# Two transformer blocks on one Trainium2 core: loads of weights, modulation and a transform matrix in another order around the merge and down stages

## What is computed

```python
mod = silu_c @ w_mod[layer] + b_mod[layer]
sh1, sc1, g1, sh2, sc2, g2 = [m[:, None, :] for m in jnp.split(mod, N_MOD, axis=-1)]
h = modulate(rms_norm(x, norm1_w[layer]), sh1, sc1)
q, k, v, g, f = split_proj(h @ wi)
o, _, _ = bidir_retention(q, k, v, a_f, a_b, s_f, s_b)
# fourier_mix: z = fft2(f as (l, 4, 128), axes=(1, 3), norm='ortho').real, then z @ w_four_out
y = merge_branches(h, ret_readout(o, g, w_ret_out[layer]),
                   fourier_mix(f, w_four_out[layer]),
                   w_branch_gate[layer], b_branch_gate[layer], w_out[layer])
# merge_branches: gates = sigmoid(h @ w_bg + b_bg); (g_r * ret_d + g_f * four_d) @ w_out
x = x + g1 * y
h2 = modulate(rms_norm(x, norm2_w[layer]), sh2, sc2)
x = x + g2 * conv_ffn(h2, w_up[layer], conv_w[layer], conv_b[layer], w_down[layer])
# conv_ffn: u = depthwise_conv3(h @ w_up); a, val = split(u); (gelu(a) * val) @ w_down
```

## Time and profile before

| | |
|---|---|
| median of 3 runs | 2527.25 us (2525.51 to 2527.36) |
| profiled execution | 2529.91 us, span 2528.1 us |
| mean granted TensorE clock | 0.965 of full |
| PE busy | 2333.3 us, 92% |
| DVE, ACT, POOL busy | 896.2 us (35%), 618.4 us (24%), 133.9 us (5%) |
| chain that ended last | PE 72%, DMA 20%, DVE 4%, ACT 2% |
| data moved | 570.11 MB, mean 226 GB/s |

### The profile page before, as it was taken

The page is one execution under the profiler, slowest core; times in us unless marked ns, Lnnn a source line. Parts: engine busy times, 40 slices in busy tenths (PEclk is TensorE's granted clock), DMA queues, the critical chain, the costliest instruction groups (busy, mean ns, idle before and its releaser), DMA issues.

```text
span 2528.1 us, 25780 instructions
## 1 busy us (share of the span) xinstructions
PE 2333.3 (92%) x11168; PEld 1525.9 (60%) x11168; DVE 896.2 (35%) x1177; ACT 618.4 (24%) x873; POOL 133.9 (5%) x128
## 2 busy tenths in 40 slices
PE   6999999999998999998999997998988989898988
PEld 5874878777886787876668786433343434343434
DVE  4837445535677424544642433010100000010102
ACT  5215133233333225414542321000000000000001
POOL 0221000110000002120000020000000000000000
PEclk8999999999999999999999997999999999999998
DMA  7220445325455222220002234999999999999993
GB/s 266 100 78 1 148 142 184 108 100 175 158 200 200 101 100 102 99 75 34 1 1 100 100 133 170 415 428 428 427 428 428 428 428 427 428 428 428 428 428 167
DMA packets 116823, 570.11 MB, mean 226 GB/s; under 512 B 5390, under 2 KB 28215, under 8 KB 92135
## 3 DMA queue, kind: packets, MB, share of 16 engines
q1 hardware_dynamic: 115104, 564.21, 55.7%
q0 software_dynamic: 1200, 4.13, 0.5%
q10 hardware_dynamic: 407, 0.13, 0.0%
HBM read 566.35 MB, written 2.10 MB: 225 GB/s over the span
## 4 chain that ended last, share of the span: by engine, by line
PE 72%; DMA 20%; DVE 4%; ACT 2%; issue 1%; POOL 1%; ACTq 0%; SPq 0%; DVEq 0%; POOLq 0%
PE ps L755 42%; DMA arena<-in_w_exp_up 9%; PE ps L1285 8%; PE ps L1348 6%; DMA arena<-in_w_exp_gate 6%; PE ps L1268 3%; DMA weights<-in_w_exp_gate 2%; PE ps L1171 1%; PE ps L1189 1%; DMA arena<-in_w_exp_down 1%; PE ps L1129 1%; PE ps L992 1%; PE ps L1300 1%; PE ps L1148 1%; DMA weights<-in_w_mod 1%
## 5 line engine op out<-in xcount | busy, mean ns | idle before, releaser
L755 PE MATMUL ps<-weights_r 128*128 128x512 f32 (+1 forms) x2784 | 861.9, 389 | 14.8 <-DVE weights_r L1874 5.0
L755 PEld LDWEIGHTS ps<-weights_r 128*128 128x128 f32 x2784 | 522.3, 189 | 128.6 <-issue 16.9
L755 PE MATMUL ps<-hT_r,weights_r 128*128 128x512 f32 x1264 | 463.0, 391 | 0.5 <-DVE weights_r L1874 0.5
L1285 PE MATMUL ps<-weights,arena 128*64 128x512 f32 x768 | 353.5, 617 | 60.1 <-DMA weights<-in_w_exp_up 46.3
L1287 PE MATMUL ps<-weights,arena 128*64 128x512 f32 x768 | 354.3, 618 | 0.0
L1874 DVE TENSOR_TENSOR weights_r<-weights,weights_r 128x4096 fp32r<-128x4096 f32 (+1 forms) x47 | 201.5, 4288 | 284.2 <-ACT weights_r L1433 282.4
L1285 PEld LDWEIGHTS ps<-weights,arena 128*64 128x64 f32 x768 | 105.9, 142 | 288.4 <-issue 286.5
L755 PEld LDWEIGHTS ps<-hT_r,weights_r 128*128 128x128 f32 x1264 | 238.6, 189 | 51.9 <-issue 2.2
L1433 ACT ACTIVATE weights_r<-weights 128x4096 fp32r<-128x4096 f32 (+1 forms) x47 | 165.3, 3518 | 339.5 <-PE ps L755 144.2
L755 PE MATMUL ps<-arena_r,weights_r 128*128 128x512 f32 (+1 forms) x640 | 228.6, 394 | 15.0 <-DVE weights_r L1874 15.0
L2473 DVE TENSOR_TENSOR hT<-hT,ps 128x512 f32<-128x512 f32 x32 | 22.0, 688 | 464.0 <-PE ps L1287 464.0
(11 more groups left out here) (290 smaller groups left out, 2511.5 us busy)
## 6 DMA issues: line engine op xcount, KB each, us to landing
weights<-in_w_exp_gate SPq DMA_DIRECT2D x48, 2048.0 KB, 23.1
weights<-in_w_exp_up SPq DMA_DIRECT2D x48, 2048.0 KB, 27.1
weights<-in_w_exp_down SPq DMA_DIRECT2D x48, 2048.0 KB, 27.0
weights<-in_w_in SPq DMA_DIRECT2D x18, 2048.0 KB, 7.9
arena<-in_w_exp_gate SPq DMA_DIRECT2D x16, 2048.0 KB, 27.6
arena<-in_w_exp_up SPq DMA_DIRECT2D x16, 2048.0 KB, 28.5
arena<-in_w_exp_down SPq DMA_DIRECT2D x16, 2048.0 KB, 28.4
weights<-in_w_mod SPq DMA_DIRECT2D x12, 2048.0 KB, 8.1
```

The lines of the kernel that those rows point to most:

```text
L755: last = pe.matmul(t, a if w_first else b, b if w_first else a, start=(k == 0 and n == 0), stop=(k == kt - 1 and n == len(pairs) - 1))
L1285: la = pe.matmul(bank(b0 + n)[0:64, :], xe[:, 2 * j + r, 0:64], wa[:, r, n * 512:(n + 1) * 512], start=start, stop=stop)
```

## The change

1. *DFT matrix.* It is no chunk any more. POOL loads it to a place of its own in the arena (`dft_cols`), ahead of the small matrix; PE waits for both before `fa` instead of for the small one before `z`. `prepare("dft")` goes on ACT and DVE.
2. *Modulation chunks of the merge.* Chunk 6 + i stands behind gate chunk i (before: 6 ahead of the first, then 7 + i), 10 behind out1's first chunk, 11 behind its second. DVE sums chunk 6 + i in the step in which PE turns it; PE turns 10 after tile 3 of out1 and 11 after tile 6.
3. *out1 and second norm.* ACT rounds up chunk 0 after the square of tile 4, and does the SiLU of the second block's modulation after that of tile 6. DVE's residual tiles, sums, columns and `prepare` are ordered anew. Up chunk 1 is rounded and subtracted in two halves right after the norm's scale (`half_high`, `half_low`, which now serve in2's chunk 1 too).
4. *Down.* Modulation chunk 11 of the second block stands behind down chunk 0, so down 0 stands directly behind modulation 10 and is split with the last up chunk. The first `act_rest` is done within the last up step.
5. The experts' first loads take the slots in the order in which the last chunks are spent.

```diff
@@ -158,7 +158,7 @@
                 b.add((tag, kind, part, nq, n), "A" if kind == "gate" else "D")
-            if tag == "m1" and i < 5:
+            if tag == "m1" and i < 4:
                 b.add(("mod1", "T", 6 + i), "D")
...
@@ -213,8 +213,8 @@
         b.add(("out1", n), "D")
-        if n == 3:
-            b.add(("mod1", "T", 11), "D")
+        if n in (3, 6):
+            b.add(("mod1", "T", 10 + (n == 6)), "D")
     norm("n2")
...
@@ -413,30 +413,28 @@
         mod1(5)
-        chunk("dft", dft_len)
-        mod1(6)
         for i, (kind, part, nq) in enumerate(MERGE):
...
             if kind == "gate":
-                mod1(7 + i)
+                mod1(6 + i)
         def mod2(i):
...
             chunk(("out1", nq), kmaj(w_out[0], 512 * nq, 512 * nq + 512))
-            if nq == 0:
-                mod1(11)
+            mod1(10 + nq)
         for j in range(UPN):
...
             mod2(j)
-        mod2(11)
         for j in range(6):
...
                 chunk(("down", j), part)
+                if j == 0:
+                    mod2(11)
             else:
...
@@ -486,7 +483,7 @@
 
-        last_tile = {"dft": ("fa", 3, 1), ("down", 5): ("cT2", 3),
+        last_tile = {("down", 5): ("cT2", 3),
                      ("in1", 0): ("qk1", 3), ("in1", 1): ("qk1", 7), ("in1", 2): ("v", 0, 3),
...
@@ -589,6 +587,7 @@
         dftd = at(13312, 2, P)
+        dft_cols = at(14336, 2, 768)
 
...
@@ -715,9 +714,9 @@
             load(0, SLOTS)
-            for m in range(RAW):
-                wait_spent(sp, NCH - RAW + m)
-                load(0, m)
+            for n in range(NCH - RAW, NCH):
+                wait_spent(sp, n)
+                load(0, n % RAW)
             for i in sorted(range(len(split) - 2, len(split)), key=high_slot):
...
@@ -923,11 +922,13 @@
                 if tag == "out1":
-                    mod_turn("mod1", 11)
+                    mod_turn("mod1", 10)
                 else:
...
                     feature_tiles((tag, 1), [(tag, n)], x, c0=n % 4 * P)
+                    if tag == "out1" and n == 6:
+                        mod_turn("mod1", 11)
                     for k in {4: (0, 1, 2), 5: (3,), 6: (4,), 7: (5,)}[n]:
...
@@ -1032,18 +1033,17 @@
             mod_turn("mod1", 4)
-            wl = slots[landed(pe, "dft")][:, 0:1536].rearrange("p (m n) -> p m n", m=2)
+            pe.wait_ge(S["dist_in"], 64)
             for g in range(FG):
...
                         o = c0 if k < 2 else 256
-                        last = pe.matmul(t[:, o:o + n], f_tok[:, k, g * P:(g + 1) * P], wl[:, m, c0:c0 + n],
+                        last = pe.matmul(t[:, o:o + n], f_tok[:, k, g * P:(g + 1) * P], dft_cols[:, m, c0:c0 + n],
                                          start=(k != 3), stop=(k != 2))
...
             mod_turn("mod1", 5)
-            pe.wait_ge(S["dist_in"], 48)
             for g in range(FG):
...
@@ -1431,6 +1429,19 @@
                     A(slots_r[high_slot(i)][:, 0:n], slots[sl][:, 0:n], ACT.Copy).then_inc(S["high_ready"], 1)
+
+            def half_high(kind, i, q):
+
+                at_split = split.index(chunk_at[kind, i])
+                if q == 0:
+                    landed(act_e, (kind, i))
+                    wait_spent(act_e, split[at_split - 2])
+                c = slice(q * SLOT // 2, (q + 1) * SLOT // 2)
+                A(slots_r[high_slot(at_split)][:, c], slots[split[at_split] % RAW][:, c], ACT.Copy).then_inc(
+                    S["quarter_high"], 1)
+                if q == 1:
+                    act_e.wait_ge(S["quarter_high"], QUARTERS[kind, i] + 2)
+                    act_e.sem_inc(S["high_ready"], 1)
 
...
@@ -1625,13 +1635,22 @@
             prepare(("out1", 0))
-            act_e.wait_ge(S["mod_summed"], summed_mods("mod1", 11))
-            mod_silu(3)
-            prepare(("out1", 1))
-            norm_squares(2, "n2", xT, L, lambda k: wait_freed(act_e, ("out1", k)))
+            def between_out1(k):
+
+                if k == 4:
+                    prepare(("out1", 1))
+                if k == 6:
+                    act_e.wait_ge(S["mod_summed"], summed_mods("mod1", 11))
+                    mod_silu(3)
+                    A(small[:, 1:2], eps_col, ACT.Sqrt)
+
+            norm_squares(2, "n2", xT, L, lambda k: wait_freed(act_e, ("out1", k)), after=between_out1)
             act_e.wait_ge(S["mods_ready"], 2)
...
                         h_parts[0], 2)
+            half_high("up", 1, 0)
+            half_high("up", 1, 1)
+            issued[0] += 1
             mod_rows("mod2", 0)
...
@@ -1673,19 +1692,7 @@
                 if q == 3:
-                    act_e.wait_ge(S["quarter_high"], 4)
-                    act_e.sem_inc(S["high_ready"], 1)
-
-            def second_high(q):
-
-                if q == 0:
-                    landed(act_e, ("in2", 1))
-                    wait_spent(act_e, split[first_in2 - 1])
-                c = slice(q * SLOT // 2, (q + 1) * SLOT // 2)
-                A(slots_r[high_slot(first_in2 + 1)][:, c], slots[split[first_in2 + 1] % RAW][:, c], ACT.Copy).then_inc(
-                    S["quarter_high"], 1)
-                if q == 1:
-                    act_e.wait_ge(S["quarter_high"], 6)
+                    act_e.wait_ge(S["quarter_high"], QUARTERS["in2", 0] + 4)
                     act_e.sem_inc(S["high_ready"], 1)
...
@@ -1875,6 +1882,18 @@
 
+            def half_low(kind, i, q):
+
+                at_split = split.index(chunk_at[kind, i])
+                ve.wait_ge(S["quarter_high"], QUARTERS[kind, i] + q + 1)
+                c = slice(q * SLOT // 2, (q + 1) * SLOT // 2)
+                sl = split[at_split] % RAW
+                last = ve.tensor_tensor(slots_r[sl][:, c], slots[sl][:, c],
+                                        slots_r[high_slot(at_split)][:, c].bitcast(F32), ALU.subtract)
+                if q == 1:
+                    ve.wait_ge(S["high_ready"], at_split + 1)
+                    last.then_inc(S["low_ready"], 1)
+
             def low_h(nth, k, high, low, src):
...
@@ -2019,13 +2038,12 @@
                         if i < 4:
-                            mod_sum("mod1", 7 + i)
-                        if i < 5:
+                            mod_sum("mod1", 6 + i)
                             mod_columns("mod1", 6 + i)
...
                 if tag == "m1":
-                    mod_sum("mod1", 11)
+                    mod_sum("mod1", 10)
 
...
@@ -2044,9 +2062,15 @@
                 if tag == "out1":
+                    mod_columns("mod1", 10)
+                    residual([(tag, 4)], 16, cc, 4)
+                    mod_sum("mod1", 11)
+                    residual([(tag, n) for n in (5, 6)], 16, cc, 5)
+                    prepare((tag, 1))
                     mod_columns("mod1", 11)
-                else:
-                    free("rbias", "D", ve.tensor_copy(route_bias, wait_full(ve, "rbias")[:, 0:NE]))
+                    residual([(tag, 7)], 16, cc, 7)
+                    return
+                free("rbias", "D", ve.tensor_copy(route_bias, wait_full(ve, "rbias")[:, 0:NE]))
                 residual([(tag, 4)], 16, cc, 4)
...
@@ -2168,8 +2192,6 @@
             mod_columns("mod1", 4)
-            prepare("dft")
-            mod_sum("mod1", 6)
             mod_columns("mod1", 5)
...
@@ -2180,6 +2202,9 @@
             norm_scale(2, "n2", xT, hT, L, split_h=(2, *h_parts))
+            half_low("up", 1, 0)
+            half_low("up", 1, 1)
+            issued[0] += 1
             def act_rest(k0):
...
@@ -2201,6 +2226,8 @@
                         prepare(("up", j))
+                    if (j, n) == (UPN - 1, 1):
+                        act_rest(0)
                 wait_freed(ve, ("up", j, 3))
...
@@ -2208,7 +2235,6 @@
                     mod_columns("mod2", j - 1)
-            act_rest(0)
             mod_columns("mod2", 10)
...
@@ -2555,6 +2570,7 @@
             po.wait_ge(S["g_ready"], KT)
+            po.dma_start(dft_cols[:, :, :], dft_len).then_inc(S["dist_in"], 16)
             po.dma_start(dftd[:, :, :], dft_dim).then_inc(S["dist_in"], 16)
...
             def sum_squares(m):

```

More of the change, by code:

```diff
@@ L451, in build_two_blocks @@
         order = {n: name for name, n in chunk_at.items()}
-        assert NCH % RAW == 0
         split = [n for n, name in enumerate(chunk_at)
@@ L546, in build_two_blocks @@
         first_in2 = split.index(chunk_at["in2", 0])
+        QUARTERS = {("up", 1): 0, ("in2", 0): 2, ("in2", 1): 6}
         root, recip = small[:, 40:44], small[:, 44:48]
@@ L1398, in norm_root, with norm_squares @@
                 copy_out(tag, root[:, 0:width // P], ACT.Sqrt, width=width // P, bias=bias)
-            def norm_squares(m, tag, src, width, written=None, between=None):
+            def norm_squares(m, tag, src, width, written=None, after=None):
                 A(small[:, 4:5], eps_col, ACT.Sqrt)
-                square_tiles(m, src, width, written)
-                if between:
-                    between()
+                square_tiles(m, src, width, written, after=after)
```

(19 more changed lines are left out.)

## The result

Over 20 runs each, the changed kernel takes 2530.57 us (2527.38 to 2534.33), the kernel before 2526.98 us (2522.68 to 2530.65): ratio 1.0017, 95% interval 1.001 to 1.0024, that is +4.3 us (+2.5 to +6.1; the two medians as they stand differ by 3.6). The direction is the one forecast and the measured time lies in the range; but the size, forecast as +8.0, is about half, and at 0.17% it is a difference that the forecast's own bound of 0.2% calls none.

A forecast was written before the change was run, and what follows sets the result against it. PE bounds the kernel, busy for most of the span and waiting for weights at full DMA rate in the second block's experts. Terms 3.4 + 8.0 + 9.4 − 3.7 − 9.1 = +8.0 give 2535.3 us, range 2526.5 to 2542.5.

The forecast's parts named there:

- A: First block's DFT: wait before turn 5 goes, a wait before the DFT comes; +3.4 us, bounds +1.5 and +7.
- B: Merge, turn 7: PE waits 5.5 us for its sum, plus 2.5 for the clock; +8.0 us, bounds +5 and +8.5.
- C: Merge, turn 9: PE waits for its sum, projection b0 starts later; +9.4 us, bounds +8 and +10.5.
- D: Second norm and up: modulation chunk 0 lands late, up chunk 1's wait goes; −3.7 us, bounds −5 and −0.5.
- E: Down stage: down chunk 0 loaded earlier, PE's wait before it shrinks; −9.1 us, bounds −8 and −10.
- rival 2: No change: gate b0 3 us sooner, clock not falling for so short a wait; total +0.8 us, 2528.0; chance 0.15.
- The rule on issuing engines: DMA transfers begun by different engines share the same 16 engines; the matrix load by POOL adds 1.8 us to gate a0.
- The forecast's case: Whole kernel slower by +4.5 to +12 us, around the term sum of +8.0; chance 0.64.
- The rival of quick pairs: Faster: the second load of each pair lands within some 9 us; sum −8.5 us, median 2518.7; chance 0.10.
- Rival 3: Slower still: slow stretches last through z, halves of up 1 wait for a load; +14.8 us, 2542; chance 0.09.
- rival 4: DFT matrix, asked for late by POOL, lands after 315 and fa waits for it; another +5 us; chance 0.02.

The follow-up runs named there:

- turns one step later: Changed kernel with turns and columns of modulation 6 to 9 one merge step later; ratio 0.9953 to the kernel before, −16.2 us against the changed kernel.
- filling the waits: Changed kernel with added matmuls keeping PE at work before turns 7 and 9; ratio 0.9994 to the kernel before, −5.8 us against the changed kernel.
- the last kernel of the experiments: Kernel before with down 0 early, up 1 in halves, DFT matrix loaded by POOL, modulation 6 ahead of gate a0; 2504.76 us, ratio 0.9908.
- the kernel with both repairs: Changed kernel with turns of modulation 6 to 9 one merge step later and gate a0 split behind the f tiles; ratio 0.9913 to the kernel before.
- Down alone: Kernel before with only the down part: modulation 11 behind down chunk 0, first lows of act within the last up step; ratio 0.9961, −9.9 us.

## Why the prediction was right in direction and too large

**The places** were all right: a wait before the DFT, before turn 7 and before turn 9, none before turn 5 and up chunk 1, a shorter one before down 0. No other wait of PE in these parts changed by more than about 1.4 us.

**A** is the term that was mis-sized most: +1.4, not +3.4. Gate a0 was ready 0.6 us sooner than worked out (issued 278.45, landed 293.81, 15.4 us; I had 14.2 + 1.8 = 16.0), and DVE's pieces behind it took 0.2 us less. The 14.2 was counted from the issue of the pair's first load (353.60); gate b0 itself was issued at 354.55 and landed after 13.25 us. The larger part is the step "It starts it behind a long wait: +2.5". The chain of the changed kernel:

```profile
278.45 15.34 DMA weights<-in_w_branch_gate
293.81 3.64 ACT weights_r L1431
...
309.75 12.99 PE ps L1043 x64
322.74 0.79 PE ps L835 x8
```

The granted clock was at 0.50 well before the wait ended (0.50 over 304.00 to 309.70) and back at full by about 314 (0.94 over 314 to 316). Under it, PE first ran the four matmuls of the DFT's first piece, which take tokens that are ready sooner, while DVE did the last sums of f (to 311.52). A slow clock there costs nothing. The main piece began at 311.58 and ended with the DFT at 322.74: 11.2 us, where it took 9.88 in the kernel before. That is 1.3 us, not 2.5. The wait was counted up to the main piece and the clock's loss whole behind it: the same microseconds twice.

**B and C** were right within 0.4 us (+8.4 and +9.3), in the mechanism too: the turns one step later bring back 16.2 us, filling the waits brings 2.4 and 2.5. That sum 8 would be ready in time is right as well.

**D** came out at −4.9, not −3.7. The up chunks took 43.98 us together against the 44.8 worked out, since the slow stretch was over with the wait and the step for modulation 0 (clock 0.51 over 559.90 to 566.30, 0.99 over the two chunks). And that step began 8.0 us after out1's end (554.77 to 562.73), where 8.4 were assumed for the load alone. PE waited 1.43 us for POOL's squares instead of 2.08, but that gained nothing, since the load ended last. That the new order of squares costs nothing is right.

**E** was −8.4, not −9.1: DVE's last pieces behind up chunk 10 ended at 828.6 and PE began at 828.9, where the same sum, shifted by 11.5 us with the rest, gives 828.1. The wait of 7.5 us in the prediction doesn't follow from its own sum (14.98 − 9.1 = 5.9); 6.64 was measured. The down stage itself was 0.8 us shorter, which the sentence "so the slow stretch behind it stays and is no gain" had at 0: in the 8 us from the start of the down stage the clock was 0.74, against 0.64 before, since less of the slow stretch was left when the wait ended.

Two slips don't change the forecast: A's lower bound is +1.6, and rival 2 adds up to +0.6, not +0.8.

So the term sum was +8.0 and the traces show +5.9, with errors of −2.0 (A), +0.4, −0.1, −1.2 (D) and +0.7 (E), which partly cancel (rounded); the down stage brings it to +5.1, and the runs say +4.3 with a width of 1.8 us on each side. What lies between the last two isn't resolved.

**The rule on issuing engines** (the Trainium skill, "DMA: Bandwidth & Descriptors", section "Issuing engines are not separate DMA queues"): POOL issued the matrix at 280.26, 1.8 us behind gate a0, and gate a0 took 15.36 us from issue to landing against 14.00 for b0, which had only one load beside it. In the six profiled executions that have both pairs, gate a0 took 15.1 to 15.4 us and b0 14.0 to 14.4: the trace agrees with the rule, and the matrix (with the small one behind it) cost gate a0 about 1.1 us, not 1.8. No run has gate a0 in this place without the matrix, so this is a comparison of two pairs. By it, on a path of its own the matrix would have left the wait about 1 us shorter.

**The chances.** The forecast's case began at +4.5, the measured difference is +4.3 with +6.1 as upper end; 0.18 for "no difference" was too little for a sum of five terms of both signs, each with an error of one or two microseconds, whose result stood only 3 us above the bound. That the difference came out so small is not rival 2's doing: the waits before turns 7 and 9 were met in full and paid for. The rival of quick pairs is out: from its own issue, gate b0 as second of a pair took 13.2 to 14.4 us in the nine executions that have that pair, and down chunk 0 13.9. Rival 3 is out (clock 1.00 over z, up chunk 1 split in time), and so is rival 4: the matrix landed 7.6 us after POOL issued it at 280.26, long before the DFT.

## What to carry to other kernels

An engine's instruction that waits for another's sum should be placed where that sum is done by the latest load ahead of it, not where its number fits: shifting turns by one step was worth 16 us, the order of the merge's loads nothing (at the down stage, where PE waited for the load itself, moving it forward was worth most of 10 us). A wait costs its own length and the slow clock behind it, but only as far as the slow work is on the path: the clock falls within a long wait, and what of the slow stretch passes before PE's next needed work is free. Where it overlaps another wait it must not be counted again. Before moving a chunk forward in a list, look at what the splitting helper pulls ahead of whom.

## What the runs showed that was not expected

Two waits of nearly the same length, at the same instruction (the sequence behind the fifth in-projection), left different clocks. The kernel before, timeline of PE and window:

```profile
175.36 1.26 PE L984 MATMUL ps<-arena 64*128 64x512 f32 x4 [2.04 <-issue]
```

```profile
175.20:186.20 11.00, 10.84 (x34) 4.84 (x36) 6.31 (x11) 4.38 (x10) 7.96 (x15) 0.84 0.48 181
```

The changed kernel, whose program is the same there:

```profile
174.30 1.13 PE L985 MATMUL ps<-arena 64*128 64x512 f32 x4 [1.88 <-issue]
```

```profile
174.20:185.20 11.00, 10.90 (x42) 4.92 (x44) 7.36 (x12) 4.38 (x10) 8.40 (x15) 1.00 0.50 187
```

A wait of 2.04 us was followed by a slow stretch, one of 1.88 us by none, which moved all that follows by 1.7 us between two executions. It isn't the length that decides. At the same place, waits in the last kernel of the experiments and in "Turns one step later", each with its window:

```profile
175.32 2.50 PE L985 MATMUL ps<-arena 64*128 64x512 f32 x8 [1.93 <-issue]
...
175.20:186.20 11.00, 10.88 (x34) 4.86 (x36) 6.31 (x11) 4.38 (x10) 8.29 (x15) 0.84 0.49 185
```

```profile
176.05 1.99 PE L985 MATMUL ps<-arena 64*128 64x512 f32 x8 [2.42 <-issue]
...
175.90:186.90 11.00, 10.85 (x42) 4.87 (x44) 7.41 (x13) 4.38 (x10) 8.48 (x15) 1.00 0.46 177
```

The shorter of these was followed by a slow stretch, the longer by none. Over the ten profiled executions this place had a slow stretch in three (waits of 1.93, 2.04 and 2.39 us) and none in seven (1.79 to 2.42 us). The wait of 1.33 us for the lows of the branch was followed by a mean clock of 0.72 over 6 us in "Turns one step later" and in the kernel with both repairs, and by 1.00 in the kernel before, in "Down alone" and in the last kernel. What decides in these cases is open; no experiment was made on it.

From the f tiles to the down stage every wait of 4.7 us and more was followed by a slow stretch; where PE was kept at work instead, none was. The wait of 2.83 us in the changed kernel stands in one, too (0.51 over 559.90 to 566.30, in the table of windows above), but the second norm has a slow stretch in all ten executions, with or without that wait. Single executions of one kernel spread over 7 to 9 us here, so of a change of this size only parts measured within a trace, or many runs, tell anything.
